# Seven FFNs: gate and up blocks as 2x2 blocks with seven products in place of eight, their sums made by adding DMAs and by GpSimd

## The reference

```python
def swiglu(x, w_gate, w_up, w_down):
    return (jax.nn.silu(x @ w_gate) * (x @ w_up)) @ w_down
```

## Time and profile before

| | us |
|---|---|
| median of 3 runs | 2456.77 |
| lowest and highest | 2456.68, 2456.95 |
| span of the profiled execution | 2455.0 |
| instructions in the profile | 30703 |
| bytes moved | 504.42 MB, 205 GB/s as a mean |

### The profile page before, as it was taken

How to read it: one execution, slowest core, us unless ns; L and a number is a source line. 1 busy time by engine, 2 the same in 40 slices (tenths; PEclk the granted TensorE clock), 3 DMA queues, 4 the chain that set the end, 5 groups by cost and what they waited for, 6 DMA issues and landing times.

```text
span 2455.0 us, 30703 instructions
## 1 busy us (share of the span) xinstructions
PE 2426.3 (99%) x12690; PEld 2069.7 (84%) x12690; DVE 1559.7 (64%) x1629; ACT 1183.0 (48%) x1276; POOL 205.5 (8%) x358
## 2 busy tenths in 40 slices
PE   8999999999999999999999999999999999999998
PEld 6889998888889988888889878888888898788887
DVE  6555876655656776565558657656665677577664
ACT  5435544434437544444435664544344356644442
POOL 0100200100100101101100010011011000100010
PEclk9999999999999999999999999999999999999999
DMA  8755447657654447657664445476576454454762
GB/s 334 238 209 189 156 165 246 227 209 237 236 204 181 164 148 272 227 205 259 227 214 174 161 154 206 180 262 231 202 256 231 172 184 152 150 208 159 256 232 101
DMA packets 82547, 504.42 MB, mean 205 GB/s; under 512 B 11608, under 2 KB 12760, under 8 KB 30184
## 3 DMA queue, kind: packets, MB, share of 16 engines
q1 hardware_dynamic: 61488, 433.23, 49.2%
q0 software_dynamic: 19744, 67.65, 8.6%
q10 hardware_dynamic: 1176, 1.58, 0.4%
HBM read 476.72 MB, written 25.69 MB: 205 GB/s over the span
## 4 chain that ended last, share of the span: by engine, by line
PE 91%; DVE 5%; ACT 3%; issue 1%; DMA 1%; SPq 0%; POOL 0%; DVEq 0%; POOLq 0%; ACTq 0%
PE acc L615 24%; PE acc L616 24%; PE acc L617 24%; PE acc L583 4%; PE acc L584 4%; PE acc L585 4%; DVE w_lo L516 2%; PE aux L799 1%; ACT w_hi L508 1%; DMA raw<-in_w 1%; ACT tmp L1484 1%; PE stat L633 1%; PE bc L633 0%; PE aux L1170 0%; PE aux L981 0%
## 5 line engine op out<-in xcount | busy, mean ns | idle before, releaser
L516 DVE TENSOR_TENSOR w_lo<-raw,w_hi 128x2048 fp32r<-128x2048 f32 (+1 forms) x417 | 934.3, 2244 | 672.3 <-ACT w_hi L508 671.5
L508 ACT ACTIVATE w_hi<-raw 128x2048 fp32r<-128x2048 f32 (+1 forms) x417 | 782.8, 1880 | 624.2 <-PE acc L617 594.0
L615 PE MATMUL acc<-w_hi,x_hi 128*128 128x512 f32 (+1 forms) x1848 | 720.4, 390 | 3.1 <-DVE x_lo L1736 2.1
L617 PE MATMUL acc<-w_lo,x_hi 128*128 128x512 f32 (+1 forms) x1848 | 715.6, 387 | 0.0
L616 PE MATMUL acc<-w_hi,x_lo 128*128 128x512 f32 (+1 forms) x1848 | 715.5, 387 | 0.0
L615 PEld LDWEIGHTS acc<-w_hi,x_hi 128*128 128x128 f32 x1848 | 347.1, 188 | 77.8 <-issue 6.1
L617 PEld LDWEIGHTS acc<-w_lo,x_hi 128*128 128x128 f32 x1848 | 347.0, 188 | 71.3
L616 PEld LDWEIGHTS acc<-w_hi,x_lo 128*128 128x128 f32 x1848 | 347.2, 188 | 70.4 <-issue 1.0
L615 PE MATMUL acc<-w_hi,h_parts 128*128 128x512 f32 x704 | 274.5, 390 | 0.0
L617 PE MATMUL acc<-w_lo,h_parts 128*128 128x512 f32 x704 | 273.9, 389 | 0.0
L616 PE MATMUL acc<-w_hi,h_parts 128*128 128x512 f32 x704 | 273.9, 389 | 0.0
(11 more groups left out here) (396 smaller groups left out, 2229.3 us busy)
## 6 DMA issues: line engine op xcount, KB each, us to landing
raw<-in_w SPq DMA_DIRECT2D x399, 1024.0 KB, 4.8
squares<-tmp POOLq DMA_DIRECT2D x40, 512.0 KB, 2.9
tmp<-squares POOLq DMA_DIRECT2D x160, 128.0 KB, 4.5
raw<-in_w SPq DMA_DIRECT2D x18, 512.0 KB, 3.6
tmp<-in_norm_gb POOLq DMA_DIRECT2D x8, 1024.0 KB, 5.4
tmp<-in_norm_gb POOLq DMA_DIRECT2D x6, 512.0 KB, 3.7
tmp<-in_gate_rows POOLq DMA_DIRECT2D x12, 256.0 KB, 3.1
squares<-tmp POOLq DMA_DIRECT2D x8, 256.0 KB, 2.3
```

The lines of the kernel that those rows point to most:

```text
L508: nc.scalar.activation(w_hi[:, slot, 0:kind], raw[:, slot, 0:kind], ACT.Copy).then_inc(hi_done, 1)
L516: nc.vector.tensor_tensor(w_lo[:, slot, 0:kind], raw[:, slot, 0:kind], w_hi[:, slot, 0:kind].bitcast(F32), ALU.subtract).then_inc(lo_done, 1)
L615: nc.tensor.matmul(out, vh, wh, start=first and k == 0, stop=False)
L617: last = nc.tensor.matmul(out, vh, wl, start=False, stop=last_k and k == nk - 1)
```

## The change

It concerns the seven FFNs behind the first (`ffn`; the first stays as it was and is called `ffn0`). Blocks 1 to 4 are handled as two groups. In group n the gate and up chunks of block i (i = 1, then 3) are the four blocks of a 2x2 matrix of 512x512 blocks, B11 and B21 (gate, upper and lower rows) and B12 and B22 (up). x is the other 2x2 matrix: two token tiles by two halves of the features. Its product is made of seven block products with four sums of weight blocks (T1 to T4) and four sums of x blocks. Each block product (`product`) is 12 matmuls. The four chunks of block i+1 are done as before, by `both`. A group is eleven chunks in this order: T1, B11, B22, B21, T2, gate 0, T3, gate 1, T4, up 0, up 1.

The sums of weight blocks are made in `raw`. T1 is the plain load of B12 into its slot and then a DMA from POOL's queue that adds B11 to it on the way (`accum_op`). T2, T3 and T4 fall on the slots of T1, B22 and T2, where one more adding DMA makes them out of what is there. The sums of x are eight operations of 128x512 on POOL (`x_sums`) behind the norm load, split like x by ScalarE and VectorE. Three of the seven products are copied out of PSUM by ScalarE, and VectorE adds or subtracts what the four outputs are made of. HOT moves to another place in `tmp`; some semaphores are merged or renamed (not shown).

```diff
+GROUP = (((LOAD, B12), (ADD, B11)), ((LOAD, B11),), ((LOAD, B22),), ((LOAD, B21),),
+         ((ADD, B22),), ((LOAD, 4 + B11),), ((ADD, B12),), ((LOAD, 4 + B21),),
+         ((ADD, B21),), ((LOAD, 4 + B12),), ((LOAD, 4 + B22),))
+GROUPS = ((1, 4), (3, 15))
...
         def split_hi(act, c, slot, kind):
-            act.wait_ge(loaded[slot], 16 * (c // RING + 1))
+            if moves[c][-1][0] == ADD:
+                act.wait_ge(added[sums.index(c) % 2], 16 * (sums.index(c) // 2 + 1))
+            else:
+                act.wait_ge(loaded[slot], 16 * landings[c])
...
+                def product(c, bank, v_hi, v_lo, first):
+
+                    chunk_ready(c)
+                    for k in range(4):
+                        wh, wl = wblock(c % RING, k, 512)
+                        nc.tensor.matmul(bank, v_hi[:, k], wh, start=first and k == 0, stop=False, skip_group_check=True)
+                        nc.tensor.matmul(bank, v_lo[:, k], wh, start=False, stop=False, skip_group_check=True)
+                        last = nc.tensor.matmul(bank, v_hi[:, k], wl, start=False, stop=k == 3, skip_group_check=True)
+                    last.then_inc(chunk_done, 1)
+
+                def group(g, b, tile):
+
+                    a_, b_, e_ = aux[:, 0, :], aux[:, 1, :], bc[:, :]
+                    x11, x12, _, x22 = ((x_hi[:, k, at], x_lo[:, k, at]) for k, at in X_AT)
+                    s1, s3, s2, s4 = zip(SUM_HI, SUM_LO)
+                    pe.wait_ge(sum_parts, 4 * (f - 1) + 1)
+                    if b:
+                        pe.wait_ge(outs_ready, 3 * b - 2)
+                    product(g + G_T1, e_, *s1, True)
+                    if b:
+                        pe.wait_ge(kept_silu, 2 * b)
+                    product(g + G_B11, b_, *x11, True)
+                    pe.wait_ge(sum_parts, 4 * f)
+                    pe.wait_ge(kept_copied, 3 * b + 1)
+                    product(g + G_B22, e_, *s4, False)
+                    if b:
+                        pe.wait_ge(outs_ready, 3 * b - 1)
+                    product(g + G_B21, a_, *x12, True)
+                    pe.wait_ge(kept_copied, 3 * b + 2)
+                    product(g + G_T2, b_, *s2, False)
+                    both(g + G_GATE0, tile, 0)
+                    pe.wait_ge(kept_copied, 3 * b + 3)
+                    product(g + G_T3, b_, *s3, False)
+                    both(g + G_GATE1, tile, 1)
+                    pe.wait_ge(outs_ready, 3 * b + 3)
+                    product(g + G_T4, b_, *x22, False)
+                    both(g + G_UP0, tile + 2, 0)
+                    both(g + G_UP1, tile + 2, 1)
...
 @block.scalar
+                def sum_high(q):
+                    act.wait_ge(sum_ready, 4 * (f - 1) + q + 1)
+                    nc.scalar.activation(SUM_HI[q], XQ4[SUM_AT[q]], ACT.Copy).then_inc(sum_hi, 1)
+
+                def kept(g, b, i):
+
+                    ended_chunk(act, g + G_T1)
+                    act.wait_ge(sum_parts, 4 * f)
+                    if i > 1:
+                        act.wait_ge(hid_ready, 12 * f + 2 * (i - 2) + 2)
+                    nc.scalar.activation(Q5B, bc[:, :], ACT.Copy).then_inc(kept_copied, 1)
+                    ahead.to(g + 4)
+                    ended_chunk(act, g + G_B11)
+                    nc.scalar.activation(P1B, aux[:, 1, :], ACT.Copy).then_inc(kept_copied, 1)
+                    ahead.to(g + 5)
+                    if i > 1:
+                        hid_high(i - 2)
+                    ahead.to(g + 7)
+                    ended_chunk(act, g + G_T2)
+                    nc.scalar.activation(UB, aux[:, 1, :], ACT.Copy).then_inc(kept_copied, 1)
+                    ahead.to(g + 9)
...
+                def ups():
...
+                    silu(0, 0)
+                    if s:
+                        sum_high(0)
+                    ahead.to(c0 + 4)
+                    if s:
+                        for q in range(1, 4):
+                            sum_high(q)
+                    silu(0, 1)
+                    ahead.to(c0 + 7)
+                    if s:
+                        for n, (i, g) in enumerate(GROUPS):
+                            kept(c0 + g, 2 * (f - 1) + n, i)
...
 @block.vector
+                def kept(g, b, i):
+
+                    ahead.to(g + 4)
+                    if i > 1:
+                        hid_low(i - 2)
+                    ahead.to(g + 7)
+                    dve.wait_ge(kept_copied, 3 * b + 3)
+                    V_.tensor_tensor(UB, bc[:, :], UB, ALU.subtract).then_inc(outs_ready, 1)
+                    ahead.to(g + 8)
+                    ended_chunk(dve, g + G_B21)
+                    dve.wait_ge(kept_copied, 3 * b + 2)
+                    V_.tensor_tensor(P1B, P1B, aux[:, 0, :], ALU.add).then_inc(outs_ready, 1)
+                    ahead.to(g + 9)
...
+                def ups():
...
+                    times(0, 0)
+                    if s:
+                        sum_low(0)
+                        ahead.to(c0 + 4)
+                        for q in range(1, 4):
+                            sum_low(q)
+                    ahead.to(c0 + 6)
+                    times(0, 1)
+                    turn_squares(0)
+                    ahead.to(c0 + 7)
...
 @block.gpsimd
+            def add(c):
+
+                how, place = moves[c][-1]
+                if len(moves[c]) > 1:
+                    pool.wait_ge(loaded[c % RING], 16 * landings[c])
+                else:
+                    pool.wait_ge(lo_done, c - RING + 1)
+                pool.dma_start(raw[:, c % RING, 0:WIDE], t[f"w{WIDE}"][place], accum_op=ALU.add)\
+                    .then_inc(added[sums.index(c) % 2], 16)
+
+            def x_sums():
+
+                def whole(q):
+                    k, at = X_AT[q]
+                    gc(G_.tensor_tensor(XQ4[q], x_hi[:, k, at].bitcast(F32), x_lo[:, k, at].bitcast(F32), ALU.add))
+
+                whole(2)
+                whole(3)
+                gc.settle()
+                G_.tensor_tensor(XQ4[3], XQ4[2], XQ4[3], ALU.subtract).then_inc(sum_ready, 1)
+                whole(0)
+                gc.settle()
+                pool.wait_ge(sum_ready, 4 * (f - 1) + 1)
+                G_.tensor_tensor(XQ4[2], XQ4[0], XQ4[2], ALU.subtract).then_inc(sum_ready, 1)
+                whole(1)
+                pool.wait_ge(sum_ready, 4 * (f - 1) + 2)
+                G_.tensor_tensor(XQ4[0], XQ4[3], XQ4[0], ALU.subtract).then_inc(sum_ready, 1)
+                gc.settle()
+                pool.wait_ge(sum_ready, 4 * (f - 1) + 3)
+                G_.tensor_tensor(XQ4[1], XQ4[1], XQ4[0], ALU.add).then_inc(sum_ready, 1)
...
+                    if s:
+                        add(c0 + 4 + G_T1)
                     pool.wait_ge(x_parts, 4 * (s + 1))
                     load_norm(s + 1)
...
+                    x_sums()
+                    add(c0 + 4 + G_T2)
+                    add(c0 + 4 + G_T3)
+                    permute(f, 0)
+                    add(c0 + 4 + G_T4)
+                    add(c0 + 15 + G_T1)
+                    add(c0 + 15 + G_T2)
+                    permute(f, 1)
+                    add(c0 + 15 + G_T3)
+                    permute(f, 2)
+                    add(c0 + 15 + G_T4)
+                    for i in range(3, 6):
+                        permute(f, i)
```

More of the change, by code:

```diff
@@ L38, with transfers @@
 CROSS = [WIDE] * 8
[L39 to L42, removed]
+FFN0 = [WIDE] * (UP_CHUNKS + 5) + [HALF] * 2 + [WIDE] * 5
+FFN = [WIDE] * (UP_CHUNKS + 6 + 5) + [HALF] * 2 + [WIDE] * 5
+SUBS = ["ffn0", "mix1", "ffn"] + ["ffn", "mix1", "ffn"] + ["ffn", "mix2", "cross", "ffn"] * 2
+KINDS = {"ffn0": FFN0, "ffn": FFN, "mix1": MIX1, "mix2": MIX2, "cross": CROSS}
+TILES = {"ffn0": 26, "ffn": 18, "mix1": 30, "mix2": 46, "cross": 10}
+LOAD, ADD = "load", "add"
+B11, B21, B12, B22 = range(4)
+GROUP = (((LOAD, B12), (ADD, B11)), ((LOAD, B11),), ((LOAD, B22),), ((LOAD, B21),),
+         ((ADD, B22),), ((LOAD, 4 + B11),), ((ADD, B12),), ((LOAD, 4 + B21),),
+         ((ADD, B21),), ((LOAD, 4 + B12),), ((LOAD, 4 + B22),))
+G_T1, G_B11, G_B22, G_B21, G_T2, G_GATE0, G_T3, G_GATE1, G_T4, G_UP0, G_UP1 = range(11)
+GROUPS = ((1, 4), (3, 15))
+def transfers():
+    out, place = [], {WIDE: 0, HALF: 0, LAT: 0}
+    for sub in SUBS:
+        kinds, j = KINDS[sub], 0
+        while j < len(kinds):
+            kind, n = kinds[j], 1
+            if sub == "ffn" and j in (4, 15):
+                n = len(GROUP)
+                out += [[(how, place[kind] + at) for how, at in moves] for moves in GROUP]
+                place[kind] += 8
+            else:
+                out.append([(LOAD, place[kind])])
+                place[kind] += 1
+            j += n
+    return out
 def wide(w):
@@ L218, in __init__ @@
             c = base[s]
[L219 to L222, removed]
+            if kind == "ffn0":
+                for i in range(5):
                     self.block(c + 4 * i + 1)
@@ L225, in __init__ @@
                 for last in (c + 21, c + 27, c + 33):
```

(24 more changed lines are left out.)

231 lines of the change are left out of this document (152 added, 79 removed).

## The result

The changed kernel takes **2713.76 us** as a median of four runs (2711.39 to 2724.16), the kernel before 2456.72 on the same chip (2456.48 to 2456.95): a ratio of **1.105**, 95% interval 1.104 to 1.107. The forecast was 2471 with a range up to 2535. The sign was right, the size was wrong by a factor of eighteen: 257 us lost where 14 were forecast.

A forecast was written before the change was run, and what follows sets the result against it. TensorE, busy 2426.3 of 2455.0 us, was taken as the bound: 2455.0 - 38.1 (matmuls) + 35.7 (sums of x) + 17 (adding DMAs) = 2469.6 for the span, so 2471 us measured, range 2424 to 2535.

The forecast's parts named there:

- What is removed: TensorE, 14 groups in seven FFNs: 168 matmuls fewer at 0.2267 us each, 38.1 us saved, called certain.
- The splits in a steady group cost nothing: Second group of an FFN: VectorE's 35.5 us fit into 40.8, so the splits cost nothing.
- the other test: Sign of being wrong: waits in the second group at T2 or GATE0, where none were forecast.
- The sums of x: First group: POOL's eight sums make the splits late, TensorE delayed 5.1 us an FFN, 35.7 us in seven.
- S: Time in the third sublayer when POOL's last sum of x is ready, forecast as 388.6.
- The further 1.2 us at B21: First group: TensorE's delay, 3.9 us at B11, was to reach 5.1 us by B21.
- The clock: Rival: the new gap in each FFN slows twelve matmuls by 2.4 us, 17 in all, giving 2488; chance 0.10.
- The adding DMAs: POOL's queue, 56 adds landing in 7.2 us: T4 1.2 us late in each group, 17 us in all.
- The prediction's own sign of being wrong: The forecast is wrong if the adds land within 5 us or take over 9.
- the rival of slow adds: Adds fetched twice need 44 us a group against 40.8; 2535 at 9 us an add, 2598 at 10.8; chance 0.14.
- The formula of five us an FFN for each further us: Adding DMAs: each us of landing time above 6.6 costs five us per FFN.
- The threshold: Adding DMAs: up to 6.6 us to landing a sum, T4's lateness would be nothing.

The follow-up runs named there:

- kernel 5: Kernel 3 without POOL's eight sums of x and their splits, the products reading plain blocks of x: 2423.80 us, ratio 0.987.
- kernel 9: One-group kernel (blocks 3 and 4 of each FFN) with T1 to T4 as plain SyncE loads, sums of weight blocks left out: 2436.60 us, ratio 0.992.
- kernel 3: Changed kernel with T1 to T4 as one plain load each from SyncE's queue, no adding DMAs, sums of weight blocks left out: 2481.59 us, ratio 1.010.
- kernel 10: One-group kernel with hidden block 2 split after the group, T1 and T2 now summed by POOL instead of adding DMAs, everything computed: 2447.62 us, ratio 0.996.
- kernel 2: Changed kernel with POOL's 56 adding DMAs as plain loads at the same places, sums of weight blocks left out: 2596.23 us.
- the 89 us of order: Changed kernel with only T4's adding DMA issued ahead of the permute in both groups: 2624.66 us, 89 less than the change.
- kernel 6: Changed kernel with POOL's adding DMAs as plain loads and T4's issued ahead of the permute, sums of weight blocks left out: 2525.88 us.
- kernel 4: Changed kernel with B11 and B22 split ahead of the last three sums of x on ScalarE and VectorE, adds kept: 2711.97 us.

## Why the prediction failed

**What is removed: right.** 12522 matmuls against 12690, and kernels 5 and 9 show the time: 33 of 38.1 and 20 of 19.0 us.

**The splits in a steady group cost nothing: nearly right.** T2 has no wait in kernels 3 and 5. GATE0, named as the other test, has short ones in the second group: 0.5 to 1.3 us four times in kernel 3, 0.3 to 0.7 us three times in kernel 5; the changed kernel has none there. A second small miss: with no add left, kernel 3 still shows 7.2 us in seven waits on L2038, six of them in first groups, behind the late sums of x (kernel 5, without these: 2.0). T4 adds to the bank that this output sum must have read, and VectorE has it behind UP0's split; I had looked at the splits alone. It grows in the changed kernel, below.

**The sums of x: right in mechanism, and in size with some luck.** POOL's timeline in the changed kernel, third sublayer:

```profile
376.28 2.56 POOL L2745 TENSOR_TENSOR tmp<-x_hi,x_lo 128x512 f32<-128x512 f32 x2
378.92 1.29 POOL L2750 TENSOR_TENSOR tmp<-tmp 128x512 f32<-128x512 f32 x1
...
388.31 1.29 POOL L2760 TENSOR_TENSOR tmp<-tmp 128x512 f32<-128x512 f32 x1
389.53 0.89 POOL L2738 DMA_DIRECT2D raw<-in_w  x1
...
397.45 0.88 POOL L2738 DMA_DIRECT2D raw<-in_w  x1 [7.03 <-DVE w_lo L572]
399.49 0.56 POOL L2723 DMA_DIRECT2D squares<-tmp  x1 [1.17 <-DVE tmp L2000]
409.57 2.29 POOL L2729 DMA_DIRECT2D tmp<-squares  x4 [9.52 <-DMA squares<-tmp]
411.85 0.98 POOL L2738 DMA_DIRECT2D raw<-in_w  x1
```

An operation takes 1.29 us undisturbed (1.37 taken; the Trainium skill's "GPSIMD Engine Reference", section 3.1, has 4497 ns for 2048 elements, and 4932 ns were measured at that size in kernel 10, so it is a little low here). The last sum ends at 389.6 against S = 388.6. Two misses partly cancel in it: eight undisturbed operations would take 10.3 us where I had 11.0, but VectorE's work beside them cost 2.8 us (one operation took 3.34) where I had 0.6. The gap at B11 is 4.52 against 3.9; the seven in this kernel are 33.8 us, against 35.7. The further 1.2 us at B21 did not show, since B11's twelve slow matmuls took 5.28 us in place of 2.72.

**The clock: the rival I gave 0.10 happened at every gap**, and it is part of the size. All 21 waits of over 4 us behind the first chunk are followed by starts 0.43 apart, as in the earlier trace rows. The rival's price, 2.4 us a gap and 17 in all, is what kernel 3 shows: 16.7 (against kernel 5). It should have been in the forecast: the earlier trace rows was the only row of the trace with a long rest, and it showed the fall; "less than half as long" was no row against it.

**The adding DMAs: the step that failed.** The text took 7.2 us to landing, one fetch more (4.8 + 2.4), and from it 1.2 us of lateness a group, 17 us in all. L2738's own instructions show 7.9 us at least, 9.3 as a median and 15.4 at most, T4's add 12.3 to 15.4 in all 14 groups, and the waits at T4 are 187.4 us. The prediction's own sign of being wrong, adds of over 9 us, came true. Laid beside the prediction's own chain, the first group of the third sublayer says where:

| step of the chain | predicted | measured | late by |
|---|---|---|---|
| T3's add issued | 397.5 | 397.45 | 0 |
| permute's store landed | 406.2 | 409.28 | 3.1 |
| T4's add issued | 409.0 to 409.5 | 411.85 | 2.9 or less |
| T4's add landed | 416.7 | 427.26 | 10.6 |
| T4 may start | 421.0 | 434.97 | 14.0 |
| T4 due (TensorE free) | 419.8 | 422.3 | 2.5 |

The store behind an add gave 3 us, T4's own add 8, and 3.4 us behind UP0's split are the sum that I had not looked at; the wait is 2.5 us shorter than that because TensorE comes late itself. The largest is T4's add, and there two things were wrong. First, the time of the engines: 5.6 us of all 16 against 2.9. I had this as the rival of slow adds ("18 MB or 44 us if each add goes through twice, more than 40.8") and gave it 0.14, though "Collectives: The Full Stack" of the Trainium skill (Part 3, the bandwidth ceiling) states it for the adding transfers of collectives and the windows had a share of 0.83 already. The two together were the argument, and I weighed each alone. Second, one landing time for all. The formula of five us an FFN for each further us gives 13 at 9.3 us; 187.4 / 7 is 26.8. The add that decides is not the median one: T4's goes out behind the permute's loads and SP's into engines that are full, and takes 15.4: its first packet starts 4.2 us after the issue (T2's add, issued at 389.53: 1.6), its packets then last 10.7 us (6.0), with a load of SP from 413.77 to 427.07 beside them.

The threshold ("up to 6.6 us a sum it would be nothing") was wrong as well: kernel 2's loads land in 5.5 as a median, and 95 us of waits remain.

**The rival of slow adds** gave 2535 at 9 us and 2598 at 10.8, and 2713.8 was measured. It was too low for the same two terms, and because the clock stood in another rival: the waits at T4 are gaps too, and 59.4 - 18.6 = 41 us of slow matmuls belong to the waits that the adds made, most of them at T4, the rest at T3 of the second group. The two rivals were one case: both make gaps, and behind every gap of over 4 us the clock was low.

**The sum again with the measured terms:** 2455.0 - 38.1 + 34.0 (the sums of x, as in kernel 3) + 187.4 (T4) + 59.4 (clock) = 2697.7. The other 12.0 are further waits for splits, 13.2 (47.2 less 34.0), less 1.2 elsewhere. Nearly all of them are at T3 of the second group, where I had none (471.70, 2.38 us, is the first); T2 and GATE0, which I had named as the test, have none in this kernel.

**Left open.** How the 89 us of order and the 118 us of adding share the engines' time with SP's ring was not taken apart further, nor was it tried to slow down SP's loads so that an add finds the engines free. The adding was replaced by POOL's own sums for two of the four sums only, in a kernel of one group an FFN (kernel 10). Why kernel 6 is 44 us above kernel 3 is argued, not shown.

## What to carry to other kernels

Price a DMA by the time that it occupies the engines, not by its landing: an accumulating transfer into SBUF took twice a plain one here, and in a stretch whose DMA share was 0.83 before, that is time which the other transfers pay. Where several transfers and small stores hang on each other in one queue, the last of them needs slack of its own; put what TensorE waits for ahead of what it doesn't. And count each new gap of a few microseconds on TensorE with the slow matmuls behind it, here 16.7 us on top of 34.0 of waiting.

## What the runs showed of the hardware that was not expected

- An adding DMA of 1 MB occupies all 16 engines for 5.6 us against 2.9 for a load (packets of 8 KB: 629 ns against 309), and its issue holds POOL for 0.92 us as a mean against 0.55 for the same transfer without adding (kernel 2).
- The profile gives an add the bytes and packets of a plain load: 263 GB/s at a DMA share of 1.03. A full share with few bytes is how it shows itself. That the time left over is the fetch of what stands in SBUF fits, but isn't shown.
- A 512 KB store directly behind an add on the same queue lands in 10.4 us as a median (28 stores), 4.8 behind a plain load (kernel 2), 2.9 in the kernel before.
- POOL and VectorE slow each other: 1.29 us becomes 3.35 for POOL's 128x512, 2.29 becomes 3.07 for VectorE's 128x2048. "SBUF — State Buffer" of the Trainium skill (section "Who interferes with whom") says that a VectorE operation with two inputs from SBUF and GpSimd's reads contend; kernel 4 agrees, with a size.
- The granted clock fell to 1.2 GHz behind all 21 waits of over 4 us; behind the one of 2.38 us it stood at 0.57 as well (471.70 to 475.70). At 1004.10 the first two matmuls still started fast, and the ones from the third on were 0.43 apart. Shorter waits went both ways: in kernel 4 one of 1.90 us (471.32) was followed by starts 0.43 apart, one of 3.16 us (614.05) was not.
